# Cached values loaded as four neighbouring tokens per partition, cached keys with every fourth token in one quarter of the partitions

## The reference, cut to what matters

```python
k_past = cache_k[j][page_table].reshape(Bs, 1024, 8, 128)   # 8 sequences, 8 pages of 128 tokens each
v_past = cache_v[j][page_table].reshape(Bs, 1024, 8, 128)
gate_scores = einsum('bhqd,bnhd->bhqn', q, mean of k over blocks of 256 tokens)
# of the 4 past blocks the 3 with the highest gate score are kept, and the block of the new tokens
s = einsum('bhqd,bhqnkd->bhqnk', q, k_kept) * DH**-0.5 - slope[h] * (q_pos - k_pos)
o = einsum('bhqnk,bhqnkd->bhqd', softmax(s), v_kept)
```

## Time and profile before

| what | us |
|---|---|
| median of 3 runs | 681.06 |
| lowest and highest | 679.63, 681.30 |
| the profiled execution's own time | 683.59 |
| its span (first to last record of the trace) | 681.80 |

### The profile page before, as it was taken

The page is one execution under the profiler, slowest core; times in us unless marked ns, Lnnn a source line. Parts: engine busy times, 40 slices in busy tenths (PEclk is TensorE's granted clock), DMA queues, the critical chain, the costliest instruction groups (busy, mean ns, idle before and its releaser), DMA issues. The chain is left out here.

```text
span 681.8 us, 11125 instructions
## 1 busy us (share of the span) xinstructions
PE 630.5 (92%) x4237; PEld 381.0 (56%) x4237; DVE 361.2 (53%) x707; ACT 216.7 (32%) x460; POOL 197.7 (29%) x222
## 2 busy tenths in 40 slices
PE   6789999999999999989999999999997996979996
PEld 5647656664666466644444556677744464554541
DVE  3232837483747465637420543345759977387422
ACT  4235233524262425201100515554152243431010
POOL 0032127022802180402000158999801020200000
PEclk9869999999999999989999999999998997979998
DMA  9996374887596658894894463354999999999991
GB/s 306 375 391 239 124 247 153 311 307 247 202 332 243 242 198 327 295 382 164 300 341 150 152 229 124 137 200 140 350 379 401 349 408 409 408 401 408 360 391 42
DMA packets 82193, 190.28 MB, mean 279 GB/s; under 512 B 4119, under 2 KB 12583, under 8 KB 82012
## 3 DMA queue, kind: packets, MB, share of 16 engines
q1 hardware_dynamic: 80484, 183.70, 73.3%
q0 software_dynamic: 1120, 4.46, 1.7%
q10 hardware_dynamic: 536, 1.41, 0.6%
HBM read 167.14 MB, written 22.41 MB: 278 GB/s over the span
## 5 line engine op out<-in xcount | busy, mean ns | idle before, releaser
L511 POOL TENSOR_TENSOR weights_low<-ring,weights_high 128x512 fp32r<-128x512 f32 x80 | 100.6, 1297 | 58.9 <-PE bank L704 47.1
L715 PE MATMUL bank<-weights_high,h_high 128*128 128x512 f32 x272 | 109.3, 402 | 0.0
L715 PE MATMUL bank<-weights_high,h_low 128*128 128x512 f32 x272 | 106.9, 393 | 0.0
L1263 ACT ACTIVATE weights_high<-ring 128x1024 fp32r<-128x1024 f32 x72 | 74.1, 1054 | 86.4 <-PE bank L723 78.9
L723 PE MATMUL bank<-weights_low,h_high 128*128 128x512 f32 x272 | 82.5, 401 | 0.9 <-DVE weights_low L511 0.9
L715 PEld LDWEIGHTS bank<-weights_high,h_high 128*128 128x128 f32 x272 | 51.2, 188 | 26.4 <-issue 15.1
L1758 DVE TENSOR_TENSOR partial_low<-bank,partial_high 128x512 fp32r<-128x512 f32 x26 | 17.9, 688 | 87.7 <-ACT partial_high L1218 60.6
L1923 DVE STREAM_TRANSPOSE ring<-ring 128x1024 f32<-128x1024 f32 x48 | 55.4, 1211 | 10.4 <-DMA ring<-in_cache_k 10.4
L683 PE MATMUL bank<-ring,arena 128*128 128x512 f32 x128 | 58.3, 594 | 0.0
L723 PEld LDWEIGHTS bank<-weights_low,h_high 128*128 128x128 f32 x272 | 49.9, 188 | 14.2 <-DVE weights_low L511 3.9
L715 PEld LDWEIGHTS bank<-weights_high,h_low 128*128 128x128 f32 x272 | 51.2, 188 | 11.1
(11 more groups left out here) (244 smaller groups left out, 960.7 us busy)
## 6 DMA issues: line engine op xcount, KB each, us to landing
ring<-in_w_ada SPq DMA_DIRECT2D x12, 2048.0 KB, 13.5
ring<-in_cache_k SPq DMA_DIRECT2D x48, 512.0 KB, 8.3
ring<-in_cache_v SPq DMA_DIRECT2D x40, 512.0 KB, 10.8
ring<-in_w_ret_in SPq DMA_DIRECT2D x8, 2048.0 KB, 11.9
ring<-in_state_ret SPq DMA_DIRECT2D x32, 512.0 KB, 9.1
out_state_sample<-ring SPq DMA_DIRECT2D x32, 512.0 KB, 6.3
ring<-in_w_moba_in SPq DMA_DIRECT2D x8, 2048.0 KB, 8.5
arena<-in_cache_v SPq DMA_DIRECT2D x24, 512.0 KB, 10.3
```

The lines of the kernel that those rows point to most:

```text
L511: tensor_tensor(w_low[:, slot, k, :], ring[:, slot, k * CH:(k + 1) * CH], high[:, k, :].bitcast(F32), ALU.subtract).then_inc(low_ready[LOW ...
L715: pe.matmul(o[i][:, :], xs[p][i][:, k, :], high[:, k, :], start=k == 0 and p == 0, stop=False)
L1263: nc.scalar.activation(w_high[u[0] == "moba"][:, 2 * i:2 * i + 2, :].rearrange("p a b -> p (a b)"), w[:, 2 * i * CH:(2 * i + 2) * CH], ACT ...
```

## The change

Value pages: partition m (every fourth of the slot) now gets tokens 4 m to 4 m + 3, which are neighbours in memory, as one piece of 16 KB. Key pages: partition 32 i + m now gets token 4 m + i, so that the scores' row blocks agree with the values; the destination is written as before as 128 partitions, the source as four groups of 32 rows, 16 KB apart in a group. The distances in the table `alibi` follow: the token of column m and block i is at 128 page + 4 m + i. No instruction of a computing engine is added or removed.

```diff
-    kpos = (np.arange(PAGES)[:, None] * P + np.arange(32)[None, :]).reshape(-1)
-    put("alibi", -slope[:, None] * (PAST + q[:, None] - kpos[None, :] - 32 * ii[:, None]))
+    kpos = (np.arange(PAGES)[:, None] * P + 4 * np.arange(32)[None, :]).reshape(-1)
+    put("alibi", -slope[:, None] * (PAST + q[:, None] - kpos[None, :] - ii[:, None]))
...
                 elif kind == "k":
                     for j in range(4):
-                        src = t["cache_k"][0, bass.ds(page[a][4 * b + j], 1)].rearrange("o p h d -> (o p) (h d)")
+                        src = t["cache_k"][0, bass.ds(page[a][4 * b + j], 1)].rearrange(
+                            "o (p i) h d -> (o i) p (h d)", i=4)
                         sp.dma_start(slot[:, j * D:(j + 1) * D], src).then_inc(got, 16)
...
                     for j in range(4):
                         src = t["cache_v"][0, bass.ds(page[a][4 * b + j], 1)].rearrange(
-                            "o (i p) h d -> (o p) i (h d)", p=32)
-                        sp.dma_start(slot[j:P:4, :].rearrange("p (i n) -> p i n", i=4), src).then_inc(got, 16)
+                            "o (p i) h d -> (o p) (i h d)", i=4)
+                        sp.dma_start(slot[j:P:4, :], src).then_inc(got, 16)
```

## The result

The changed kernel takes 931.09 us (median of 4 runs, 928.15 to 934.3) against 680.38 us for the kernel before on the same chips: 1.367 times, 95% interval 1.362 to 1.373. The profiled execution took 928.15 us, its span is 926.3 us. The forecast was 903 with a range of 880 to 940: the four engines were foreseen rightly, the size came out 28 us short.

The account below looks back on a forecast made before the run. DMA engines bound the kernel from the first key page on, four of them after the change: 441.2 + 413.3 - 1.5 + 2.5 = 855.5, + 47.7 = 903.2 us span; forecast 903 us, range 880 to 940.

Parts of the forecast that it names:

- Engines by the outermost count: Key page DMAs: largest number up to 16 dividing both outermost counts, so 4 engines and 5.14 us instead of 1.285.
- The same four for every page: Key pages: assumed all 64 use the same four engines, so each costs the full 5.14 us.
- Rivals 1 and 2: Key pages stay at 1.285 us, 679.3 us, chance 0.10; or four engines differing by page, 683 us, chance 0.04.
- Never dry: Four engines' stream from first keys to values 5: no gap charged, up to 10 us in the range.
- Values in one piece: Value pages as 16 KB rows: 0 to 3 us saved, 1.5 taken; SyncE's shorter issue counted as nothing.
- the first of the sum: 64 key pages on four engines at 5.14 us each, 329.0 us.
- what the four engines carry besides keys: Value pages 61.7 less 1.5 us, three weight units 16.8, new keys and values written out 5.8.
- first and last byte: First issue to first byte and last byte to semaphore, around the four engines' stream: 2.5 us.
- from there to the end: From values 5 landed to the kernel's end: 44.7 us before, 47.7 predicted.
- a slow clock: TensorE leaving a long idle stretch after values 5: 0.9 us more for scores, 2 for what stands around them.
- Rival 3: Four engines disturb each other writing 32 adjacent partitions: key pages at half rate, 329 us more, about 1230; chance 0.02.

Follow-up runs that it names:

- the adjacent values: Kernel with only the values in one piece, but each value page written to 32 adjacent partitions instead of every fourth: 761.7 us, 1.118 times the kernel before.
- the far groups: Kernel before with only a key page's source changed to 16 groups of 8 rows, 64 KB apart in a group: 719.7 us, ratio 1.056.
- the near ones: Kernel before with a key page's source as 16 groups of 8 neighbouring rows, one row left out between groups: 715.3 us, ratio 1.049.

## Why the prediction was right, and where 28 us went

*Engines by the outermost count: right.* 4, 8 and 16 groups gave 12, 8 and 0 missing completions a page.

*The same four for every page: right.* Four pages under way at a time would fill all 16 if they rotated; the share beside keys alone is 0.26 throughout. Rivals 1 and 2 are out.

*Never dry: right, though not as argued.* From 750 to 755 and 815 to 820 us, while SyncE still waited to issue keys 6 and 7, the engines moved 107 and 92 GB/s, all of it values and weights, with no key packet in either window: the backlog covered the wait, longer than I had counted since it drained more slowly. I had charged no gap, and none of note shows.

*Values in one piece: not contradicted,* 1.5 us taken, 1.7 measured by itself, with an interval of the ratio that goes from nothing to 0.5%. SyncE's issue fell from 602 ns to 543 only, and it is hidden.

*The term that was mis-sized* is the first of the sum, the key pages at 64 x 5.14 = 329.0 us. It takes one price for a key page whatever goes beside it. Alone a page costs the four engines 4.9 us, less than that; beside values and weights its packets take nearly twice as long, and that was put at nothing. The second, smaller, is what the four engines carry besides keys, 61.7 - 1.5 + 16.8 + 5.8 = 82.8 us. The reckoning from the first key page to values 5 landed (TensorE's wait for them, answering to the earlier trace rows):

```profile
884.50 1.91 PE L1038 MATMUL bank<-ring,arena 128*8 128x256 f32 x32 [1.18 <-DMA ring<-in_cache_v]
```

| | predicted | measured |
|---|---|---|
| first key page issued | 441.2 | 436.5 |
| 64 key pages | 329.0 | 354 (64 x 4.9 = 313.6, and 40 of slowed packets) |
| everything else on the four engines | 82.8 | 92 (what is left) |
| first and last byte | 2.5 | 2.0 (1.5 from issue to first packet, 0.5 from last completion to TensorE) |
| values 5 landed | 855.5 | 884.5 |
| from there to the end | 47.7 | 41.8 |
| span | 903.2 | 926.3 |

So 25 us too little for the keys and 9 for the rest, against 4.7 too much for the start, 0.5 for the first and last byte and 5.9 for the tail, where I had added 3 us for a slow clock that was back at 2.4 GHz (PEclk 1.00) from 885 us on: together 23 us of span. Against the median it is 28, since the profiled execution was the fastest of its runs and that of the kernel before lay 2.5 us above its median. That the result fell inside the range owes something to luck: without the slowing the same sum would have been about 26 us too high (15 in the keys, the rest in start, ends and tail), and that made up for half of what was missed.

The 40 us come from the durations of the packets: 1253 of 8192 key packets took over 200 ns (median 286) against 159 for the others, all but a few in the stretches with values or weights beside them. What the remaining 9 us are is not separated. Rival 3 named something like it (engines that disturb each other on 32 adjacent partitions) but would have had it all the time: keys alone on four engines are not slowed, 26.7 GB/s an engine; keys with something beside them are, to 59 GB/s for the four, and so is what goes beside them. The row that I held against it, values on every fourth partition at 408 GB/s, spoke of 16 engines that write to spread partitions, not of these. That the slowing in the changed kernel itself is the port conflict which the adjacent values show is argued from the same signature (full share, half the rate); no run took it away there, so this cause stays open.

One reading of the prediction was off without bearing on the sum: slice 29 of the earlier trace rows begins at 477 us, not at 494.

No version tried beats the kernel before by more than a measurement tells; the values in one piece would need keys in the matching order, and each way tried of loading keys in that order costs 52 us or more.

## What to carry to other kernels

Before reshaping a DMA, look at the outermost count of both sides: in every shape tried here the number of engines was the largest up to 16 that divides both, and packets minus data rows in the profile's queue rows tells how many engines completed. A transfer on few engines can be dearer than its bytes on those engines: price it with what goes beside it. A full DMA share is not a full rate: share and GB/s have to be read together, and a share of 1.0 at half the usual rate pointed to where the engines write in the one kernel that tested it alone. Splitting a transfer to get the engines back costs issue time on the queue, here 0.5 to 0.8 us a DMA, which for 128 KB is longer than the move (0.32 us at 408 GB/s).

## What the runs showed of the hardware that was not expected

- With key pages on four engines and transfers on all 16 side by side, both are slowed: a 4 KB key packet from 159 to 286 ns, a 16 KB value packet from 611 to about 1070 ns, 15 to 16 GB/s an engine at a full share (26.7 for keys alone).
- 16 engines writing to 32 adjacent partitions reach 212 GB/s at a share of 0.99; to 32 partitions four apart, 426.
- 16 groups against 128 rows uses all 16 engines and is still slower (322 GB/s for the far groups and 319 for the near ones from 560 to 580 us) than 128 against 128 (408).
- SyncE is held in the issue while the engines of its DMA are behind: median 4.64 us a key page, up to 12.8, instead of 0.33.
- Reading 4 KB rows 16 KB apart costs nothing: 408 GB/s, 679.7 us.
